# Second feed-forward product as seven block products per unit, and a token-major output projection

## The chip, the cores and the metric

One core of one Trainium2 chip runs the whole layer as one program. The metric is the device time in microseconds (us) of that program; lower is better. The engines are TensorE (PE in the profile; PEld its weight loads), VectorE (DVE), ScalarE (ACT), GpSimd (POOL) and SyncE (SP), which issues most of the DMAs.

## The reference

The layer takes x (512 tokens by 1024 features, float32) and 25 weight tensors. Cut to what matters here:

```python
h = x * (1 + sc1) + sh1                      # modulation from c, w_ada
p = h @ w_in                                 # pool, RWKV and gate columns
y_pool = pool_branch(p_pool, ...); y_rwkv = rwkv7_branch(p_rwkv, ...)
g_pool, g_rwkv = split(sigmoid(p_gate))
mixed = (g_pool * y_pool + g_rwkv * y_rwkv) @ w_out
x = layer_norm(ALPHA * x + (1 + gt1) * mixed, ln1_g, ln1_b)
h = x * (1 + sc2) + sh2
f = square(relu(h @ w_ff1)) @ w_ff2          # 1024 -> 4096 -> 1024
x = layer_norm(ALPHA * x + (1 + gt2) * f, ln2_g, ln2_b)
```

## The kernel before, in words

Activations lie feature-major in SBUF: 128 features on the partitions, 512 tokens (S) along the free axis, KT = 8 such tiles for 1024 features. Float32 precision is made from three products of a reduced format: each operand is split into a high part (ScalarE copies it to the format) and a low part (value minus high part), and hi x hi, hi x lo and lo x hi are added in one PSUM bank. So one column block of 128 outputs over 1024 inputs is 8 x 3 = 24 matmuls of 128 x 512.

The weights come in chunks k = 0, 1, ... of 128 x (8 x 128), 512 KB each, listed in `srcs`. For each chunk SyncE issues the load into `w_raw` (`load_chunk`, L401), ScalarE writes `w_hi` (`split_hi`, L641, and `split_again`, L942), GpSimd writes `w_lo` (`split_lo`, L560, L616), TensorE multiplies (`product`, L1773), and the semaphores `w_in*`, `hi_ready`, `lo_ready`, `w_used` carry it along; three or four slots are used in turn. K_UP is the first chunk behind the scan, K_OUT the first of w_out, K_FF the first of the feed-forward part.

Every engine works through its own instructions in the order written; each instruction also raises a semaphore that its own engine then waits for (`link`). The stages, one after the other:

- The input projection and the chunked RWKV scan, QUADS rounds of 27 slots (to about 520 us). At its end VectorE makes y.
- Mixing: for each of 8 column blocks the gate columns, the RWKV up product and the pool up product; VectorE combines them in four operations and splits off `mix_lo`. Before the first block come four small `mix_pool` matmuls, which wait for ScalarE's `pool_scaled`.
- The output projection, feature-major: 8 blocks of 24 matmuls (w_out is the stationary operand). x is loaded again (`x_again`) and turned to feature-major by 32 transposes between the blocks; `take_product` adds gate times product to `res`, and VectorE and ScalarE sum values and squares as they come.
- First layer norm over features, thus over partitions: matmuls with a matrix of ones give the sums (`token_sums`, L1837), `spread` (L1854) brings mean and deviation back to all partitions, VectorE subtracts and multiplies (L1356, L1357), ScalarE makes h and its high part (L932, L933), GpSimd the low part (L611). `first_products` (L1875) starts on it.
- Feed-forward, four quarters q of 1024 hidden features: 8 chunks of w_ff1 give 8 hidden tiles (ScalarE: relu L951, high part of the square L952; VectorE: square L1371 and low part L1373), then 8 chunks of w_ff2 multiply them, and VectorE adds gate times product to `res` (L1378). The middle quarters are a loop.
- In the last quarter each finished tile of `res` is turned back to token-major (`turn_back`, L1761), ScalarE copies it out (L959), VectorE takes statistics, and the second layer norm is applied in token-major (L1404, L1406; one of the four token blocks by ScalarE and GpSimd). Four stores of 512 KB end the program.

## Time and profile before

| | us |
|---|---|
| median of 3 runs | 1096.57 |
| lowest, highest | 1090.94, 1103.49 |
| profiled execution: its own time | 1097.87 |
| profiled execution: span of the instructions | 1096.1 |
| TensorE busy in the span | 995.9 |
| VectorE, ScalarE, GpSimd busy | 520.8, 413.7, 402.4 |

The span runs from the first to the last instruction of the profiled execution; the time also holds what lies around it. Busy times of matmuls overlap, since each one is pipelined behind the other, so the spacing of their starts tells the rate. DVE, ACT and POOL rows name the instruction's line, the tile written and the tiles read; "set" and "bank" are PSUM.

### The profile page before, as it was taken

The numbers are of one execution on the slowest core, as the hardware profiler recorded it, in microseconds if no ns is written. First come the engines' busy times: TensorE is split into PE (matmuls) and PEld (weight loads), VectorE is DVE, ScalarE is ACT, GpSimd is POOL, SyncE is SP. The second block draws the span as 40 slices with busy tenths as digits, with TensorE's granted clock in tenths as the row PEclk, the third lists the DMA queues.
The fourth block names the chain that finished last, engine by engine and source line by source line (L and its number), as shares of the span: only waits on it lengthen the run. The fifth ranks groups of instructions, "written<-read, shape, count | busy, mean of one in ns | idle before, by whom it ended". The sixth has DMA issues, their size and how long they took to land.

```text
span 1096.1 us, 25425 instructions
## 1 busy us (share of the span) xinstructions
PE 995.9 (91%) x10997; PEld 798.7 (73%) x10997; DVE 520.8 (48%) x620; ACT 413.7 (38%) x500; POOL 402.4 (37%) x236
## 2 busy tenths in 40 slices
PE   1798999798989899899899999899999999999992
PEld 1676777685768578766688888678888888888881
DVE  5735688466837867853431246745112112112217
ACT  0336355345435623335432224384124224214311
POOL 6332512310231131125454444355444444443422
PEclk9698999998999999999999999889999999999996
DMA  9332333233222423422443543304333333333201
GB/s 363 103 90 62 97 102 100 61 83 119 86 79 80 119 65 99 116 86 59 135 115 87 165 123 96 96 5 130 97 96 97 96 96 96 96 96 96 77 1 77
DMA packets 153641, 108.08 MB, mean 99 GB/s; under 512 B 5395, under 2 KB 145601, under 8 KB 153537
## 3 DMA queue, kind: packets, MB, share of 16 engines
q1 hardware_dynamic: 143729, 83.46, 26.0%
q10 hardware_dynamic: 9808, 23.08, 6.9%
q8 instruction: 84, 1.38, 0.5%
q14 instruction: 20, 0.16, 0.0%
HBM read 100.23 MB, written 2.10 MB: 93 GB/s over the span
## 4 chain that ended last, share of the span: by engine, by line
PE 75%; DVE 14%; ACT 3%; DMA 2%; issue 2%; POOL 1%; ACTq 1%; SPq 1%; DVEq 0%; POOLq 0%
PE set L1773 23%; PE bank L1773 20%; PE bank L1476 12%; PE set L1518 3%; PE set L1530 2%; PE set L1542 2%; PE bank L1457 2%; PE set L1554 1%; PE bank L1875 1%; DMA ptab<-in_mu_shift_dram 1%; DVE y L1280 1%; DVE Q L1038 1%; PE set L1565 1%; DVE Q L1057 1%; PE set L1875 1%
## 5 line engine op out<-in xcount | busy, mean ns | idle before, releaser
L560 POOL TENSOR_TENSOR w_lo<-w_raw,w_hi 128x1024 fp32r<-128x1024 f32 (+2 forms) x87 | 201.7, 2318 | 441.2 <-ACT w_hi L641 401.1
L616 POOL TENSOR_TENSOR w_lo<-w_raw,w_hi 128x1024 fp32r<-128x1024 f32 x48 | 115.8, 2412 | 145.6 <-ACT w_hi L942 145.4
L1476 PE MATMUL bank<-h_hi,w_hi 128*128 128x512 f32 x256 | 109.3, 427 | 2.2 <-POOL w_lo L560 2.0
L669 ACT ACTIVATE Q<-set 128x1024 f32<-128x1024 f32 x56 | 57.4, 1025 | 135.1 <-PE set L1530 75.6
L641 ACT ACTIVATE w_hi<-w_raw 128x1024 fp32r<-128x1024 f32 (+2 forms) x75 | 75.5, 1006 | 83.0 <-PE set L1773 43.5
L942 ACT ACTIVATE w_hi<-w_raw 128x1024 fp32r<-128x1024 f32 x60 | 63.7, 1061 | 110.7 <-PE bank L1773 53.9
L1476 PE MATMUL bank<-h_lo,w_hi 128*128 128x512 f32 x256 | 104.1, 407 | 0.0
L1476 PE MATMUL bank<-h_hi,w_lo 128*128 128x512 f32 x256 | 103.5, 404 | 0.6 <-issue 0.6
L1371 DVE TENSOR_TENSOR f<-t 128x512 f32<-128x512 f32 x32 | 26.3, 823 | 125.6 <-ACT t L951 125.2
L1773 PE MATMUL set<-y_hi,w_hi 128*128 128x512 f32 x192 | 76.2, 397 | 0.0
L1773 PE MATMUL bank<-h_hi,w_hi 128*128 128x512 f32 x192 | 75.9, 395 | 0.0
L1773 PE MATMUL bank<-h_hi,w_lo 128*128 128x512 f32 x192 | 75.3, 392 | 0.0
L1773 PE MATMUL bank<-h_lo,w_hi 128*128 128x512 f32 x192 | 75.3, 392 | 0.0
L1773 PE MATMUL set<-y_lo,w_hi 128*128 128x512 f32 x192 | 75.3, 392 | 0.0
L1773 PE MATMUL set<-y_hi,w_lo 128*128 128x512 f32 x192 | 75.1, 391 | 0.0
L1476 PEld LDWEIGHTS bank<-h_hi,w_hi 128*128 128x128 f32 x256 | 49.9, 195 | 19.2 <-issue 6.0
L1530 PE MATMUL set<-Q 64*64 64x64 f32 x2560 | 45.7, 224 | 14.8 <-issue 7.0
L1476 PEld LDWEIGHTS bank<-h_hi,w_lo 128*128 128x128 f32 x256 | 49.6, 194 | 11.1
L1530 PEld LDWEIGHTS set<-Q 64*64 64x64 f32 x2560 | 42.6, 138 | 20.5 <-issue 13.0
L1476 PEld LDWEIGHTS bank<-h_lo,w_hi 128*128 128x128 f32 x256 | 49.8, 194 | 9.0
L1773 PE MATMUL bank<-y_hi,w_hi 128*128 128x512 f32 x128 | 50.9, 398 | 0.0
L1773 PE MATMUL bank<-y_hi,w_lo 128*128 128x512 f32 x128 | 50.2, 393 | 0.0
(338 smaller groups left out, 2028.7 us busy)
## 6 DMA issues: line engine op xcount, KB each, us to landing
w_raw<-in_w_ff_dram SPq DMA_DIRECT2D x64, 512.0 KB, 3.9
w_raw<-in_w_in_dram SPq DMA_DIRECT2D x46, 512.0 KB, 3.8
y<-in_w_ada_dram ACTq DMA_DIRECT2D x20, 512.0 KB, 4.2
ada<-in_w_ada_dram SPq DMA_DIRECT2D x16, 512.0 KB, 10.0
Q<-in_w_ada_dram ACTq DMA_DIRECT2D x12, 512.0 KB, 4.3
w_raw<-in_w_rwkv_up_dram SPq DMA_DIRECT2D x8, 512.0 KB, 4.1
w_raw<-in_w_out_dram SPq DMA_DIRECT2D x8, 512.0 KB, 4.0
xtok<-in_x_dram SPq DMA_DIRECT2D x4, 512.0 KB, 10.0
```

The costliest lines, as they stand in the source:

```text
L560: link(pool.tensor_tensor(part_of(k, w_lo), part_of(k, w_raw), part_of(k, w_hi).bitcast(F32), ALU.subtract), "lo_ready")
L616: again(pool.tensor_tensor(part_of(k, w_lo), part_of(k, w_raw), part_of(k, w_hi).bitcast(F32), ALU.subtract), "lo_ready")
L641: link(act.activation(part_of(k, w_hi), part_of(k, w_raw), ACT.Copy), "hi_ready")
L669: link(act.activation(by_half(tile), psum_flat(set_of(name)), ACT.Copy), "act_kept")
L942: link(act.activation(part_of(k, w_hi), part_of(k, w_raw), ACT.Copy), "hi_ready")
L1371: link(dve.tensor_tensor(f3[:, :], r[:, :], r[:, :], ALU.mult))
L1457: mm = pe.matmul(o, w, hx, start=(m == 0), stop=(m == 3 * KT - 1))
L1476: mm = pe.matmul(o, w, hx, start=(m == 0), stop=(m == 3 * KT - 1))
L1518: mm = pe.matmul(ps[C * q:C * q + C, p, c * C:(c + 1) * C], by_head(left, p, q, c), by_head(right, p, q, c - back), start=(m == 0), stop=( ...
L1530: mm = pe.matmul(ps[N * p:N * p + N, q, c * C:(c + 1) * C], by_pair(left, p, q, c), by_pair(right, p, q, c), start=(m == 0), stop=(m == le ...
L1542: mm = pe.matmul(ps[C * q:C * q + C, p, 2 * c * C:2 * (c + 1) * C], by_head(left, p, q, HC * h + c), two_blocks(x, z, rows, q, HC * h + c) ...
L1773: mm = pe.matmul(o, w[chunks[k][1]][:, kt, :], hx[:, kt, :], start=(kt == 0 and m == 0), stop=(kt == kts - 1 and m == 2))
```

## The change

The hidden features come in 8 units u of 512 (NU) in place of 4 quarters of 1024. A unit multiplies A (512 tokens by 512 hidden) by B (512 hidden by 1024 outputs), each cut into 2 x 2 blocks: A into blocks of 256 x 256, B into B11, B12, B21, B22 of 256 x 512. In place of eight block products it makes seven, by the scheme of Strassen and Winograd: with T1 = B12 - B11, T3 = B22 - B12, T2 = B22 - T1, T4 = B21 - T2 on the weight side (VectorE, `summed`) and four sums of activation blocks (`a_sums`). Each block product is 2 rows of 128 tokens x 2 blocks of 128 hidden features x 3 terms = 12 matmuls, with the activations stationary and 512 columns of weights moving, so the result is token-major. Some products open a PSUM bank, others add onto it (`OPENS`), and VectorE adds the bank into `acc_out` at up to two points (`take`, 14 per unit).

The splitting is shared differently. Per unit ScalarE makes 11 high parts; the low parts of chunks 0, 1 and of the last four products (m = 7 to 10) are GpSimd's, those of chunks 2, 3 and products 0 to 2 (`low_tile`) VectorE's, which also makes the low parts of the activation blocks (`lows`).

The output projection becomes token-major too: `mix_hi` and `mix_lo` are stationary and w_out moves, in two halves z of 512 columns with four chunks each. Its weights are first multiplied by the first gate (`scaled_out`), which `spread_gate` brought onto all partitions as a row at the end of the scan. x is added without turning; the first layer norm is taken with bn_stats along the free axis, and the normalised x is turned to feature-major for h. The norm's gain and bias for the residual are applied block by block in units 0 to 2 (`residual`), the second gate and the final addition in unit 6 (`merged`), and in the last unit the weights carry the gate, so that the products are added straight to `res`. The result needs no turning back. More raw weight buffers exist, and the first chunks behind the scan are loaded before y is ready.

The core of the diff; the mirror definitions of buffers, the loops' counting and the removed functions are left out:

```diff
+        FORMS = ("B11", "B21", "T2", "T1", "T3", "B22", "T4")
+        NFORM = len(FORMS)
+        QUARTERS = dict(B11=(3, 0, 0), B12=(4, 0, 1), B21=(5, 1, 0), B22=(6, 1, 1))
+        FORM_RAW = dict(B11=3, B21=5, T2=3, T1=8, T3=4, B22=6, T4=5)
...
+        NU = DFF // (4 * P)
+        PER = 4 + NFORM
+        K_FORM = K_FF + 4
+        srcs += [w_cols(w_ff1, m * P) for m in range(4)] + [None] * NFORM
...
+        SLOT = (2, 0, 1, 3, 2, 0, 1, 3, 2, 0, 1)
...
+
+            raw, i, z = QUARTERS[name]
+            if u:
+                wait_low(sp, 4 + FORMS.index(LAST_FORM[name]), u - 1)
+                if name == "B11":
+                    sp.wait_ge(sem("summed"), NSUM * u)
+            elif name == "B22":
+                sp.wait_ge(sem("w_used"), K_PU[KT - 1] + 1)
+            else:
+                sp.wait_ge(sem("lo_ready"), K_OUT + {"B11": 6, "B12": 7, "B21": 5}[name] + 1)
+            src = w_ff2[0, (4 * u + 2 * i) * P:(4 * u + 2 * i + 2) * P, z * S:(z + 1) * S].rearrange("(i p) f -> p i f", p=P)
+            sp.dma_start(two_by(w_raw[raw]), src).then_inc(sem(f"w_in{raw}"), 16)
...
+        PRODUCTS = ((0, 4), (2, 0), (5, 4), (4, 6), (1, 4), (6, 6), (3, 4))
+        OPENS = (True, True, False, True, False, False, False)
+        FREED_BY = (6, None, 0, 5, 2, 3, 4)
+        READ_INTO = ((0, 0), (0, 0), (0, 1), (2, 1), (2, 1), (0, 1), (2, 0))
+        FIRST_READ = (0, 2, 3, 6)
+        OUT_BANKS = ((4, 5, 0, 1), (2, 3, 6, 7))
+        SUMS = ("T1", "T3", "T2", "T4")
+        NSUM = len(SUMS)
+        A_READY = ((1, 3), (2, 4), (5, 7), (5, 7), (6, 8), (6, 8), (6, 8))
...
+        LO_BY_DVE = (2, 3, 4, 5, 6)
+        QUARTER_ORDER = ("B11", "B12", "B22", "B21")
...
+            for k in (K_UP, K_UP + 1):
+                load_chunk(sp, k)
             sp.wait_ge(sem("y_ready"), QUADS)
...
+            load_chunk(sp, K_UP + 2)
+            for o in range(2):
+                load_out(sp, o)
...
+            for o in range(3, 6):
+                load_out(sp, o)
+            for m in (2, 0):
+                load_chunk(sp, K_FF + m)
+            load_out(sp, 6)
+            load_chunk(sp, K_FF + 1)
+            load_out(sp, 7)
+            load_chunk(sp, K_FF + 3)
+            load_quarter(sp, 0, "B22")
+            sp.wait_ge(sem("pu_taken"), KT)
+            for at, src in enumerate((ln1_g, ln1_b, ln2_g, ln2_b)):
+                sp.dma_start(ln_rows[:, at, :], src.to_broadcast([P, D])).then_inc(sem("rows_in"), 16)
+            for name in ("B21", "B11", "B12"):
+                load_quarter(sp, 0, name)
...
+            with pool.Fori(0, NU - 1) as q:
+                again = loop_link(pool, counts, q, {"lo_ready": 6}, "pool_step")
+                for m in (0, 1, 7, 8, 9, 10):
+                    pool.wait_ge(sem("hi_ready"), q * PER + (K_FF + PER + m + 1))
+                    raw = w_raw[CHUNK_RAW[m] if m < 4 else FORM_RAW[FORMS[m - 4]]]
+                    again(pool.tensor_tensor(w_lo[SLOT[m]][:, :, :], raw[:, :, :], w_hi[SLOT[m]][:, :, :].bitcast(F32), ALU.subtract), "lo_ready")
...
+                        for z, one in enumerate((gate1, gate2)):
+                            act.wait_ge(sem("gate_spread"), z + 1)
+                            link(act.activation(one[:, :], pset[(1, 0)[z]][:, :, :].rearrange("p g t -> p (g t)"), ACT.Copy, scale=(0.5, 1.0)[z]),
+                                 "gate_rows")
...
+
+            def normalise(j, stage):
+
+                act.wait_ge(sem("ln_cols"), 2 * stage + j // 2 + 1)
+                link(act.activation(res[:, j, :], res[:, j, :], ACT.Identity, scale=small[:, 36 + j:37 + j], bias=small[:, 40 + j:41 + j]), "x_hat")
+
+            root(0, 0)
+            normalise(0, 0)
+            normalise(1, 0)
+            root(1, 0)
...
+            for m in range(4):
+                relu_of(link, m, 0, 0)
+                high_raw(link, m)
+                high_sums(link, m)
+                split_hi(K_FORM + m)
...
+                x0, x1 = left[:, i, 0:S // 2], left[:, i, S // 2:S]
+                if n % 4 < 2:
+                    link(dve.tensor_tensor(a_sum[:, 0, :], x0, x1, ALU.subtract), "a_summed")
+                else:
+                    link(dve.tensor_tensor(a_sum[:, 1, :], x1, right(n)[:, S // 2:S], ALU.add))
+                    link(dve.tensor_tensor(a_sum[:, 2, :], a_sum[:, 1, :], x0, ALU.subtract))
+                    link(dve.tensor_tensor(a_sum[:, 3, :], right(n)[:, 0:S // 2], a_sum[:, 2, :], ALU.subtract), "a_summed")
...
+                raw, slot = w_raw[CHUNK_RAW[m] if m < 4 else FORM_RAW[FORMS[m - 4]]], SLOT[m]
+                link(dve.tensor_tensor(w_lo[slot][:, :, :], raw[:, :, :], w_hi[slot][:, :, :].bitcast(F32), ALU.subtract), "lo_by_dve")
...
+            def take(link, unit, at, row, units=0, into=None):
+
+                into = into or acc_out
+                wait_half(unit, at, row, units)
+                j, z = READ_INTO[at][0] + row, READ_INTO[at][1]
+                product = bank[PRODUCTS[at][1] + row]
+                if unit == 0 and at in FIRST_READ:
+                    link(dve.tensor_copy(part(into, j, z), product), "taken")
+                else:
+                    link(dve.tensor_tensor(part(into, j, z), product, part(into, j, z), ALU.add), "taken")
...
+            def merged(j, z):
+
+                link(dve.tensor_tensor(part(acc_out, j, z), part(acc_out, j, z), gate2[:, z * S:(z + 1) * S], ALU.mult))
+                link(dve.tensor_tensor(part(res, j, z), part(res, j, z), part(acc_out, j, z), ALU.add))
...
+            def residual(j, z):
+
+                link(dve.tensor_tensor(part(res, j, z), part(res, j, z), part(ln_rows, 0, z), ALU.mult))
+                link(dve.tensor_tensor(part(res, j, z), part(res, j, z), part(ln_rows, 1, z), ALU.add))
...
+                link(dve.tensor_tensor(part(res, j, z), bank[OUT_BANKS[z][j]], part(res, j, z), ALU.add), "out_taken")
+                statistics(j, z)
...
+                for at in range(NFORM):
+                    for row in range(2):
+                        take(link, unit, at, row, units)
+                    if between:
+                        between(at)
...
+            def residuals(of):
+
+                def between(at):
+                    if at in (0, 2, 4) and 3 * of + at // 2 < len(parts):
+                        residual(*parts[3 * of + at // 2])
+
+                return between
...
+            def unit_sums(link, units, last=False):
+
+                low_tile(link, 2, 1, units)
+                low_tile(link, 3, 1, units)
+                if last:
+                    for name in QUARTER_ORDER:
+                        loaded(name, 1, units)
+                        scaled_tile(QUARTERS[name][0], QUARTERS[name][2], gate2)
+                summed(link, "T1", 1, units)
+                summed(link, "T3", 1, units)
+                for m in range(4):
+                    dve.wait_ge(sem("hidden_raw"), units * 4 + (4 + m + 1))
+                    lows(link, 4 + m, units)
+                    if m == 0:
+                        low_tile(link, 4, 1, units)
+                    if m == 1:
+                        summed(link, "T2", 1, units)
+                        low_tile(link, 5, 1, units)
+                    if m == 2:
+                        low_tile(link, 6, 1, units)
+                        summed(link, "T4", 1, units)
+
+            for u in (1, 2):
+                unit_sums(link, u - 1)
+                takes(link, 1, u - 1, residuals(u))
...
+            def merges_before(at):
+                if at in (1, 4):
+                    for row in range(2):
+                        merged(READ_INTO[at][0] + row, READ_INTO[at][1])
+
+            takes(link, 1, NU - 3, merges_before)
+            unit_sums(link, NU - 2, True)
+            for at in range(NFORM - 1):
+                for row in range(2):
+                    take(link, 1, at, row, NU - 2, res)
+                if at < 4:
+                    merged(*((0, 1), (1, 1), (2, 0), (3, 0))[at])
+                if at in (1, 4, 5):
+                    for row in range(2):
+                        statistics(READ_INTO[at][0] + row, READ_INTO[at][1])
+            spreads(0)
+            for row in range(2):
+                take(link, 1, NFORM - 1, row, NU - 2, res)
+                statistics(2 + row, 0)
+                if row == 0:
+                    columns(0, 1)
...
+            def spread_gate(z, first):
+
+                for f in range(KT):
+                    mm = pe.matmul(pset[z][:, f // 4, f % 4 * P:(f % 4 + 1) * P], mod[:, first + f:first + f + 1].to_broadcast([P, P]), ident[:, :],
...
+            def quarters(unit, free, units=0):
+
+                for at, (form, first) in enumerate(PRODUCTS):
+                    wait_low(pe, 4 + at, unit, units)
+                    w = [two_by(half[SLOT[4 + at]]) for half in (w_hi, w_lo)]
+                    for row in range(2):
+                        free(at, row)
+                        if at and FREED_BY[at] is not None and FREED_BY[at] < at:
+                            pe.wait_ge(sem("taken"), units * (2 * NFORM) + (2 * NFORM * unit + 2 * FREED_BY[at] + row + 1))
+                        for i in range(2):
+                            if row == 0:
+                                pe.wait_ge(sem("a_low"), units * 8 + (8 * unit + A_READY[form][i]))
+                            for m, (a, wx) in enumerate(((a_hi, w[0]), (a_lo, w[0]), (a_hi, w[1]))):
+                                mm = pe.matmul(bank[first + row], a[:, form, i, row * P:(row + 1) * P], wx[:, i, :],
+                                               start=OPENS[at] and i == 0 and m == 0, stop=i == 1 and m == 2, skip_group_check=True)
+                        if row == 0:
+                            mm.then_inc(sem("half_made"), 1)
+                    mm.then_inc(sem("w_used"), 1)
...
+            for kt in range(KT):
+                pe.wait_ge(sem(("h2_lo_by_dve", "h2_lo_by_pool")[kt % 2]), kt // 2 + 1)
+                if kt < 4:
                     for j in range(TB):
-                        mm = pe.transpose(bank[6 + f % 2][:, j * P:(j + 1) * P], x_again[:, j, f * P:(f + 1) * P], ident[:, :])
+                        mm = turn(kt + 4, j)
...
+                slot = SLOT[m]
+                wait_low(pe, m, base, units)
+                for kt in range(KT):
+                    for at, (w, hx) in enumerate(((w_hi, h2_hi), (w_hi, h2_lo), (w_lo, h2_hi))):
+                        mm = pe.matmul(bank[m][:, :], w[slot][:, kt, :], hx[:, kt, :], start=(kt == 0 and at == 0),
+                                       stop=(kt == KT - 1 and at == 2))
+                mm.then_inc(sem("w_used"), 1)
```

## Rows read from the trace of the kernel before

**Rows 1.** the page: busy time, the chain by engine, a feed-forward weight load
```profile
PE 995.9 (91%) x10997; PEld 798.7 (73%) x10997; DVE 520.8 (48%) x620; ACT 413.7 (38%) x500; POOL 402.4 (37%) x236
...
PE 75%; DVE 14%; ACT 3%; DMA 2%; issue 2%; POOL 1%; ACTq 1%; SPq 1%; DVEq 0%; POOLq 0%
...
w_raw<-in_w_ff_dram SPq DMA_DIRECT2D x64, 512.0 KB, 3.9
```

**Rows 2.** busy time by stretch: us; busy (instructions) per engine; granted clock; DMA share, GB/s
```profile
735.00:1032.00 297.00, 297.00 (x1291) 242.66 (x1290) 69.44 (x87) 97.12 (x118) 134.63 (x56) 1.00 0.34 98
```

**Rows 3.** the chain that ended last: start us, us, what; feed-forward part
```profile
734.44 11.05 PE set L1773 x48
...
900.32 11.04 PE bank L1773 x48
```

**Rows 4.** the timeline of VectorE (DVE) and GpSimd (POOL): start us, us, instruction [idle before]
```profile
714.05 0.69 DVE L1356 TENSOR_TENSOR G<-G,set 128x512 f32<-128x512 f32 x1
...
713.56 1.27 POOL L611 TENSOR_TENSOR h_lo<-t,h_hi 128x512 fp32r<-128x512 f32 x1 [6.01 <-ACT h_hi L933]
...
738.26 2.61 POOL L616 TENSOR_TENSOR w_lo<-w_raw,w_hi 128x1024 fp32r<-128x1024 f32 x1 [0.21 <-ACT w_hi L942]
...
738.63 2.78 DVE L1373 TENSOR_TENSOR y_lo<-f,y_hi 128x512 fp32r<-128x512 f32 x1
```

**Rows 5.** the timeline of TensorE from the output projection to the first chunks
```profile
649.85 0.39 PE L1773 MATMUL set<-mix_hi,w_hi 128*128 128x512 f32 x1
...
698.29 0.39 PE L1773 MATMUL bank<-mix_hi,w_lo 128*128 128x512 f32 x1
...
705.51 2.06 PE L1854 MATMUL set<-ident,small 128*128 128x128 f32 x8
...
714.98 0.77 PE L1875 MATMUL set<-h_hi,w_hi 128*128 128x512 f32 x1 [3.92 <-POOL h_lo L611]
715.54 0.63 PE L1875 MATMUL set<-h_lo,w_hi 128*128 128x512 f32 x1
715.97 0.63 PE L1875 MATMUL set<-h_hi,w_lo 128*128 128x512 f32 x1
```

**Rows 6.** busy time and granted clock (PEclk) by slices, columns as in rows 2
```profile
704.00:706.00 2.00, 2.00 (x10) 2.00 (x11) 0.20 (x2) 1.06 (x1) 0.79 (x1) 0.50 0.00 0
...
720.00:722.00 2.00, 2.00 (x10) 1.60 (x9) 1.20 (x2) 1.90 (x4) 1.78 (x2) 0.88 0.00 0
```

**Rows 7.** the timeline of ScalarE (ACT) and TensorE at the pool mixing
```profile
533.57 1.06 ACT L641 ACTIVATE w_hi<-w_raw 128x1024 fp32r<-128x1024 f32 x1 [8.11 <-DMA w_raw<-in_w_rwkv_up_dram]
...
536.12 1.10 PE L1796 MATMUL set<-sg,wmix 128*128 128x512 f32 x2 [1.28 <-ACT lnv L882]
538.61 1.10 PE L1796 MATMUL set<-t,wmix 128*128 128x512 f32 x2 [1.40 <-ACT lnv L882]
```

**Rows 8.** groups by line and shape: count, busy us, mean ns, idle before
```profile
L616 POOL TENSOR_TENSOR w_lo<-w_raw,w_hi 128x1024 fp32r<-128x1024 f32 x48 | 115.8, 2412 | 145.6 <-ACT w_hi L942 145.4 <-POOL w_lo L616 0.2
...
L942 ACT ACTIVATE w_hi<-w_raw 128x1024 fp32r<-128x1024 f32 x60 | 63.7, 1061 | 110.7 <-PE bank L1773 53.9 <-PE set L1773 52.5 <-ACT y_hi L952 3.8
...
L951 ACT ACTIVATE t<-set 128x512 f32<-128x512 f32 x16 | 9.6, 598 | 50.0 <-PE set L1773 43.9 <-DVE y_lo L1373 3.8 <-PE set L1875 2.3
...
L1192 DVE TENSOR_TENSOR O<-O,gn 128x1024 f32<-128x1024 f32 x3 | 3.7, 1224 | 0.1
```

**Rows 9.** the timeline of TensorE at a group that turns back, last quarter
```profile
1038.21 0.60 PE L1761 MATMUL set<-ident,G 128*128 128x128 f32 x4
1038.56 0.48 PE L1773 MATMUL bank<-y_hi,w_hi 128*128 128x512 f32 x1
```

**Rows 10.** the timeline of TensorE and VectorE at the end
```profile
1073.91 0.40 PE L1773 MATMUL set<-y_hi,w_lo 128*128 128x512 f32 x1
...
1083.93 3.24 DVE L1404 SCALAR_TENSOR_TENSOR xt<-xt,small,acc 128x1024 f32<-128x1024 f32 x1
...
1091.81 1.28 DVE L1406 SCALAR_TENSOR_TENSOR xt<-xt,small,ada_late 128x1024 f32<-128x1024 f32 x1
```

727 lines of the change are left out of this document (415 added, 312 removed).

## Prediction

> **What bounds the kernel now.** I read the page first: TensorE is busy 91% of the span, and the chain that ended last lies on it for 75% [rows 1]. Then the stretches: in the 297 us from 735 it never rests [rows 2]; the timeline shows it without products only from 698.5 to 715 us (the first layer norm) and after 1074 us (the second). In the feed-forward part one piece of the chain follows another, 48 matmuls in 11.05 us, 0.2302 us each [rows 3]. So a matmul saved there is worth its whole 0.23 us, as long as the other engines feed TensorE as evenly as now. VectorE and GpSimd have room (69 and 135 us busy in those 297) [rows 2], but not independent room. A VectorE instruction of 128x512 takes 0.69 us with one operand in PSUM, and keeps that beside a running GpSimd instruction (714.05). With both operands in SBUF it took 2.78 us when it began while GpSimd ran a w_lo subtraction (738.63): it ended 0.54 us after GpSimd's. They take turns, one instruction each [rows 4]. That pair of rows decides the forecast.
>
> **The change, part by part** (base: the profiled run, 1097.87 us, span 1096.1; the median of the three runs is 1.3 below it).
>
> Scan's end: +1.0. TensorE gets 16 matmuls of 128 columns that spread two gates over the partitions. Eight such take 2.06 us at half clock [rows 5, 6], so 16 cost 2.1 (full clock) to 4.2. ScalarE's two copies of 128x1024 (1.06 each) delay y by up to as much, under the gate product. Against it, loading K_UP's weights before the wait for y takes away the DMA that ends ScalarE's wait of 8.1 us, behind which the pool mixing was late and TensorE idle 1.28 + 1.40 = 2.7 us [rows 7]. Net -0.6 to +1.5; I take +1.0, since the gate product now also waits for the first copy. Weights scaled by the first gate (8 VectorE products of 1.2 us, [rows 8] for the size) fit beside mixing, whose four VectorE operations need 2.8 of 8.3 us per column block.
>
> Output projection: -4.5. 192 matmuls stay; the 32 transposes of x and the mean's matmul leave it. It took 649.85 to 698.52, 48.7 us [rows 5]; 192 x 0.2302 = 44.2.
>
> First norm: -6.3. Now 698.52 to 714.98, 16.5 us without a product [rows 5]. After: last take 0.7 and its statistics 0.7, but ScalarE reaches the first root only after the high part of K_FF+1, which waits for the last projection matmul, so VectorE stands behind that root before the last take (+1.3); two aggregations, root, columns 1.3; the last block's normalisation 0.8; transposes 0.5, two scalings out of PSUM 1.5, high part 0.6, low part 0.7; ten hand-overs of about 0.1; ScalarE's three normalisations (1.1 to 1.3 each by the row of 128x1024 [rows 8]) lie beside it. 10.2 us.
>
> Second product: -22.1. Per unit of 512 hidden features 7 block products x 12 matmuls = 84 in place of 96; 8 units save 96 matmuls x 0.2302. The moving operand stays 512 columns wide. The page "TensorE: Matmul & The Clock Gate" of the Trainium skill, section "Wait — 56ns, not 53.3ns?", gives 215.7 ns between such matmuls at full clock; by that the saving would be 20.7 us and the sum 1.4 higher. The trace's own spacing is used.
>
> Transposes: -1.3. Each group of four costs 0.35 us, and 0.09 at the next matmul, which shows 0.48 in place of 0.39 [rows 9]; seven leave the last quarter, four come into the first chunks.
>
> Stalls in the units: +33.2. These come from laying the units' instructions out engine by engine, in the order of the code, with the durations of [rows 4, 8]. TensorE needs 22.1 us for four hidden chunks and 19.3 for seven products. Let E be the end of chunk 3. ScalarE's work per unit is 11 x 1.06 + 8 x 0.6 + 4.2 = 21 us, and fits. VectorE: 5 low tiles and 4 weight sums at 1.25, 8 differences of 128x256 at 0.45 (0.69 for 512 columns and 1.22 for 1024 leave 0.42 for 256), the low parts 5.2, 14 takes from PSUM at 0.72: 30 us of 41.4, of which 20 need SBUF twice, and GpSimd's six w_lo need 14.4 more of the same turn-taking. Four places come out late:
> (1) product 1 needs the low part of chunk 3: relu and square 0.6 each, three differences 1.35, low part 0.69 and hand-overs and the next matmul's start make about 4.1 us after E; TensorE has 15 matmuls to do until then, 3.45. Late by 0.7, in each of seven units, 2.2 in the first, where two chunks end together: 6.3.
> (2) units 0 to 2 carry two residual operations behind products 0, 2 and 4. GpSimd starts its four w_lo at E+5.4. VectorE ends the takes of product 0 at E+6.8; its first residual operation waits until E+7.9, the second until E+10.6; so the take of product 2, for which product 4 waits (same banks), is done at E+13.4, and product 4 was due at E+11.7. Late 1.7, and the same again at product 5, 1.8: 10.4 in three units.
> (3) unit 6 has four operations (gate and residual) between the takes of products 1 and 2, each behind one of GpSimd's: the take of product 2 ends at E+18, 6.3 late.
> (4) unit 7: scaling four weight quarters by the gate adds 4 x 1.25 us before T1. Behind unit 6's late takes VectorE begins 2.4 us after chunk 0 does, has 22.2 us of work before the differences of chunk 3 and waits 4 for ScalarE's high parts, so product 1 is 5.3 late; product 4 then waits 4.9 for takes behind merging: 10.2.
> Both ends: if nothing of this reached TensorE, 0; if GpSimd's turns fell as in (2) in all units, 5 x 3.5 more.
>
> Clock: +4.8. Granted clock is 1.00 until 702 us and 0.50 from 704, after the projection's matmuls had ended at 698.5, and 0.88 again in the slice from 720, dense matmuls having begun at 715 [rows 5, 6]. Those are the levels 2.4 and 1.2 GHz. At the low one matmuls start 0.43 us apart in place of 0.23 (715.54, 715.97) [rows 5]; 12 of them cost 2.4 us. The first chunks pay this now and after. The waits of 6.3 in unit 6 and 5.3 in unit 7 leave TensorE with nothing at all; I count one such fall behind each, 4.8; if the clock holds, 0.
>
> Tail: -1.3. Now the last matmul starts at 1073.91 and VectorE's last operation ends at 1093.1, with 3 us of storing behind it; the final scaling is six VectorE operations, two of them 3.24 us beside GpSimd's two [rows 10]. After, only a take, statistics of one block and the root stand before the same scaling, but takes arrive two products late: 20.4 against 21.7 us.
>
> DMA: the same 64 loads of 512 KB. Three w_ff2 quarters and four broadcast rows (2 MB) fall into the projection; a load takes 3.9 us [rows 1], so they land before T1. Its bound: if B12 were late by a load, +3.9.
> Waits: a block row of 6 matmuls has up to four semaphore waits at its head where the present loop has two per 24 matmuls, at no cost (48 matmuls in 11.05 in the loops too [rows 3]); nearest row for a price is the 0.09 us after a transpose group [rows 9]: 0 to 112 block rows x 0.09 = 10 us. I take 0.
>
> Sum: 1.0 - 4.5 - 6.3 - 22.1 - 1.3 + 33.2 + 4.8 - 1.3 = +3.5: 1101.4 on the profiled run's scale, 1100 on the median's.
>
> **Rivals.**
> *The turns cost nothing* (0.27). VectorE works 30 of 41 us, and if the residual and merging operations fall between GpSimd's, only (1), 6.3, and perhaps 4 in the last unit stay: 33.2 + 4.8 becomes about 10, time 1072. For it: takes come first in VectorE's order, and GpSimd is free half the time. Against: GpSimd's four w_lo stand back to back exactly in the products' phase, and [rows 4] show what an SBUF operation does then.
> *VectorE becomes the bound in all units* (0.26), slower. If VectorE's low tiles and sums at the head of a unit also meet GpSimd's two w_lo of chunks 0 and 1, each meeting adds up to 2.1 us to a phase with 19.7 us of VectorE work in 22.1. It decides from the point where the low part of chunk 3 is more than 3.45 us behind the matmul. 3.5 us in the five plain units: +17, time 1117. For it: the sum 19.7 + 4.8 is over 22.1. Against: GpSimd's pair is mostly done while takes run.
> The page "SBUF — State Buffer" of the Trainium skill, section "Who interferes with whom", speaks against the change here: a VectorE instruction with two SBUF inputs and a GpSimd one that reads SBUF lock each other out for a whole instruction. By it the first of these rivals would need luck in the order and the second only density. The trace agrees (2.78 against 0.69 us).
> *The saving isn't had* (0.05): the waits at each block row cost their 10 us: 1110.
>
> **How the numbers follow.** Forecast case 0.42, its own range 1088 to 1111 (stalls 33 within a third). A change within 1% of 1097, 11 us, can hardly be told from none. Faster by over 1% (below 1085.6) is the first rival and a little of the forecast: 0.30. Slower by over 1% (above 1107.5): the second, half the third, and the upper end of the forecast: 0.29. Same: 0.41. The range 1071 to 1116 leaves out the ends of both rivals.
>
> **What would show it.** Right: TensorE's matmuls in the feed-forward part fewer by 96 at 0.23 us spacing; idle before products 1, 4 and 5 with VectorE as releaser; GpSimd's and VectorE's 128x512 SBUF operations at 2.5 to 2.8 us in products' phases; unit times near 46 us for units 0 to 2, 42 for 3 to 5, about 50 for 6 and 7; about 10 us between projection and first chunk. Wrong: units of 41.5 us throughout (first rival), idle before products 1 in units 3 to 5 over 3 us (second), or spacing above 0.24 at the heads of block rows (third). A late T1, seen as VectorE waiting for DMA before it takes the projection's second half, would add to the first norm.

## The result and the profile after

The changed kernel takes 1109.72 us (median of 4; 1107.87 to 1111.28) beside 1096.05 for the kernel before on the same chip: ratio 1.0112, interval 1.0079 to 1.0146. By the ratio it is 12 us slower (9 to 16), where the forecast had 3.5. Its profiled run took 1108.20 us, with a span of 1106.3. First the page: busy time by engine, then the chain that ended last by engine.

```profile
PE 976.2 (88%) x10851; PEld 776.2 (70%) x10851; DVE 717.3 (65%) x862; ACT 462.1 (42%) x561; POOL 362.8 (33%) x218
...
PE 61%; DVE 26%; ACT 6%; issue 3%; DMA 2%; POOL 1%; ACTq 1%; SPq 0%; DVEq 0%; POOLq 0%
```

Beside [rows 1] TensorE has 20 us less to do, as intended, and VectorE 197 us more. VectorE's part of the chain went from 14% to 26%: the kernel now waits for it at places. The windows of single units show where (stretch, its length, busy time and instructions of PE, PEld, DVE, ACT, POOL, then granted clock, DMA share, GB/s).

```profile
757.00:803.00 46.00, 42.36 (x181) 33.48 (x181) 37.86 (x46) 21.13 (x28) 14.81 (x7) 1.00 0.30 92
849.00:891.50 42.50, 41.82 (x181) 33.73 (x180) 29.12 (x39) 21.22 (x27) 14.38 (x7) 1.00 0.30 89
976.60:1026.00 49.40, 42.35 (x174) 33.71 (x173) 39.01 (x42) 21.24 (x27) 13.33 (x6) 0.93 0.27 83
1026.00:1085.00 59.00, 48.14 (x187) 37.72 (x185) 55.00 (x65) 19.10 (x25) 12.86 (x5) 0.88 0.00 0
```

Unit 1, with six residual instructions, needs 46.0 us; unit 3, without, 42.5; nearly all of the difference is idle time of TensorE (3.6 against 0.7 us), which does the same matmuls. In the last window VectorE is busy 55 of 59 us. The timeline of TensorE names each wait, in brackets, with what ended it.

```profile
736.95 0.50 PE L2142 MATMUL bank<-w_hi,a_hi 128*128 128x512 f32 x1 [1.97 <-DVE a_lo L1481]
...
792.47 0.49 PE L2142 MATMUL set<-w_hi,a_hi 128*128 128x512 f32 x1 [1.49 <-DVE acc_out L1550]
...
797.01 0.51 PE L2142 MATMUL set<-w_hi,a_hi 128*128 128x512 f32 x1 [1.51 <-DVE acc_out L1550]
...
916.76 0.40 PE L2142 MATMUL bank<-w_lo,a_hi 128*128 128x512 f32 x1
917.83 0.50 PE L2142 MATMUL bank<-w_hi,a_hi 128*128 128x512 f32 x1 [0.68 <-DVE a_lo L1481]
...
1017.19 0.79 PE L2142 MATMUL set<-w_hi,a_hi 128*128 128x512 f32 x1 [6.04 <-DVE acc_out L1550]
1017.77 0.63 PE L2142 MATMUL set<-w_hi,a_lo 128*128 128x512 f32 x1
1018.20 0.63 PE L2142 MATMUL set<-w_lo,a_hi 128*128 128x512 f32 x1
...
1058.46 0.79 PE L2142 MATMUL bank<-w_hi,a_hi 128*128 128x512 f32 x1 [5.04 <-DVE a_lo L1481]
...
1073.42 0.79 PE L2142 MATMUL set<-w_hi,a_hi 128*128 128x512 f32 x1 [5.48 <-DVE res L1550]
```

These are the four places of the forecast: product 1 behind the low part of hidden chunk 3 (a_lo), products 4 and 5 behind takes, product 4 of unit 6, and products 1 and 4 of unit 7. Behind the two waits at product 4 the granted clock is at its lower level:

```profile
1018.00:1021.00 3.00, 3.00 (x8) 2.35 (x8) 1.90 (x3) 0.00 (x0) 0.00 (x0) 0.50 0.02 8
1074.00:1078.00 4.00, 4.00 (x11) 3.16 (x10) 3.79 (x7) 0.00 (x0) 0.00 (x0) 0.50 0.00 0
```

What holds VectorE is seen in its timeline beside GpSimd's.

```profile
787.39 2.78 DVE L1560 TENSOR_TENSOR res<-res,ln_rows 128x512 f32<-128x512 f32 x1
790.20 1.42 DVE L1550 TENSOR_TENSOR acc_out<-bank,acc_out 128x512 f32<-128x512 f32 x2
...
786.96 2.65 POOL L731 TENSOR_TENSOR w_lo<-w_raw,w_hi 128x1024 fp32r<-128x1024 f32 x1 [0.16 <-POOL w_lo L731]
```

The residual's addition began at 787.39 during GpSimd's subtraction, which ended at 789.61, and lasted 2.78 us; the two takes behind it, with an operand in PSUM, take 0.71 each. It is the pattern of [rows 4]. In unit 6 three of the first four merging instructions last 2.70 to 2.74 us.

**By stretches.** Marks are starts of the same matmuls in the two profiles [rows 5, 10], so each line is a difference of rows:

| stretch | before | after | change | forecast |
|---|---|---|---|---|
| until the scan's last input product ends | 516.16 | 514.49 | -1.7 | - |
| from there to the output projection | 133.69 | 133.82 | +0.1 | +1.0 |
| output projection | 48.67 | 44.33 | -4.3 | -4.5 |
| first norm, to the first chunk's first matmul | 16.46 | 12.75 | -3.7 | -6.3 |
| feed-forward, to the last matmul's end | 359.16 | 379.10 | +19.9 | +14.6 |
| from there to the span's end | 21.96 | 21.81 | -0.1 | -1.3 |

The first line is no more than scatter: in the changed kernel and its ten experiments the instructions up to the output projection are the same, and it began anywhere from 646.0 to 653.2 us in their profiles. So a single profile is read from a mark: below, "from the mark" counts from the first matmul of the output projection to VectorE's last operation, 443.2 us before (649.85 to 1093.09) and 453.7 after (648.31 to 1101.97). One part scatters behind the mark too: the first chunk starts 57.1 us behind it in every run whose first norm is unchanged, but unit 0 then takes 51.2, 51.0, 50.7 or 50.2 us in runs that do the same there (changed kernel; 3 and 4; 7; 8), as the granted clock rises and falls at different times. So a difference of 1 us can't be read from this number alone.

### The profile page after: what moved, and what is told of

It reads as the page before. It is cut to its first block, busy times and chain, and to the rows that moved or that the text cites. A ratio compares the mean times of both kernels' runs of the same rounds, so it can differ in the third digit from the quotient of the medians.

```text
span 1106.3 us, 25836 instructions
## 1 busy us (share of the span) xinstructions
PE 976.2 (88%) x10851; PEld 776.2 (70%) x10851; DVE 717.3 (65%) x862; ACT 462.1 (42%) x561; POOL 362.8 (33%) x218
## 4 chain that ended last, share of the span: by engine, by line
PE 61%; DVE 26%; ACT 6%; issue 3%; DMA 2%; POOL 1%; ACTq 1%; SPq 0%; DVEq 0%; POOLq 0%
PE bank L1797 12%; PE set L2142 7%; PE bank L2214 6%; PE set L2099 6%; PE bank L2099 5%; PE set L2214 3%; PE set L2167 3%; PE set L1839 2%; PE set L1851 2%; PE set L1863 2%; DVE w_lo L1501 2%; DVE acc_out L1550 2%; PE bank L1778 1%; DVE y L1448 1%; PE set L1875 1%
## 5 line engine op out<-in xcount | busy, mean ns | idle before, releaser
L1797 PE MATMUL bank<-h_hi,w_hi 128*128 128x512 f32 x256 | 109.7, 429 | 2.1 <-POOL w_lo L668 2.0
L1797 PE MATMUL bank<-h_lo,w_hi 128*128 128x512 f32 x256 | 104.3, 407 | 0.0
L1797 PE MATMUL bank<-h_hi,w_lo 128*128 128x512 f32 x256 | 103.6, 405 | 0.4 <-issue 0.4
L2142 PE MATMUL set<-w_hi,a_hi 128*128 128x512 f32 x192 | 78.6, 409 | 19.1 <-DVE acc_out L1550 12.1
L2142 PE MATMUL set<-w_hi,a_lo 128*128 128x512 f32 x192 | 77.4, 403 | 0.0
L2142 PE MATMUL set<-w_lo,a_hi 128*128 128x512 f32 x192 | 77.1, 402 | 0.0
L1550 DVE TENSOR_TENSOR acc_out<-set,acc_out 128x512 f32<-128x512 f32 x76 | 52.6, 692 | 23.4 <-PE set L2142 21.4
L1501 DVE TENSOR_TENSOR w_lo<-w_raw,w_hi 128x1024 fp32r<-128x1024 f32 x38 | 46.6, 1226 | 10.3 <-ACT w_hi L1113 7.6
L2214 PE MATMUL set<-h_hi,w_hi 128*128 128x512 f32 x128 | 50.6, 396 | 0.0
L2214 PE MATMUL set<-h_lo,w_hi 128*128 128x512 f32 x128 | 50.2, 392 | 0.0
```

Source lines behind the costliest of these rows:

```text
L1501: link(dve.tensor_tensor(w_lo[slot][:, :, :], raw[:, :, :], w_hi[slot][:, :, :].bitcast(F32), ALU.subtract), "lo_by_dve")
L1550: link(dve.tensor_tensor(part(into, j, z), product, part(into, j, z), ALU.add), "taken")
L1797: mm = pe.matmul(o, w, hx, start=(m == 0), stop=(m == 3 * KT - 1))
L2142: mm = pe.matmul(bank[first + row], a[:, form, i, row * P:(row + 1) * P], wx[:, i, :], start=OPENS[at] and i == 0 and m == 0, stop=i == 1 ...
L2214: mm = pe.matmul(bank[m][:, :], w[slot][:, kt, :], hx[:, kt, :], start=(kt == 0 and at == 0), stop=(kt == KT - 1 and at == 2))
```

## Experiments

Each is the changed kernel with one edit, unless said otherwise. Ratios are to the kernel before, run on the same chip; the changed kernel's is 1.0112 (1.0079 to 1.0146).

**1. Same instructions' time, one operand.**

```diff
             def residual(j, z):
-                link(dve.tensor_tensor(part(res, j, z), ..., part(ln_rows, 0, z), ALU.mult))
-                link(dve.tensor_tensor(part(res, j, z), ..., part(ln_rows, 1, z), ALU.add))
+                for _ in range(2):
+                    link(dve.bn_stats(stat[:, 2 * j + z, :], res[:, j, z * S:(z + 1) * S]))
```

> The sixteen residual instructions of units 0 to 2 (two SBUF operands, 0.69 us alone) are replaced in their places by sixteen bn_stats of the same 128x512 block, which also last 0.69 us and read one operand; the scale and the row of the first norm are so left out of the residual. Theory (turn-taking: a VectorE instruction with two SBUF operands alternates with GpSimd's 2.4 us ones): the two waits of 1.5 us at products 4 and 5 of units 0 to 2 go, these units come every 42.6 us like 3 to 5, and the time falls by 10 to 10.5 us, to about 1099. Rival (VectorE simply has 1.4 us more to do behind three products, whatever the operands): unit spacing stays near 46 us and the time at 1110.

Measured: 1098.54 us, ratio 1.0012 (0.9997 to 1.0028); from the mark 444.6, 9.1 less. Unit spacings are 42.50, 42.53, 42.53 where they were 46.1 in units 1 and 2. VectorE's timeline at the place of the residual:

```profile
787.14 1.42 DVE L1560 BATCH_NORM_STATS2 stat<-res 128x6 f32<-128x512 f32 x2
...
786.56 2.41 POOL L731 TENSOR_TENSOR w_lo<-w_raw,w_hi 128x1024 fp32r<-128x1024 f32 x1 [0.16 <-ACT w_hi L1113]
```

Two instructions in 1.42 us beside GpSimd, against 2.78 us for one. VectorE is given the same time of work; the form of the operands decides. The rival is out. (bn_stats also writes only six values a row; that this isn't the reason is seen at the takes, which write all 512, read one operand from PSUM and one from SBUF, and keep 0.71 us beside GpSimd.) The page "SBUF — State Buffer" of the Trainium skill, section "Who interferes with whom", says that a VectorE instruction with at most one SBUF input doesn't contend with GpSimd outside its two-port modes; the trace agrees.

**2. Same instructions, another place.** `takes` of units 0 to 2 lose `residuals(...)`; units 1 to 4 are written out and get two pairs each:

```diff
                     if m == 2:
                         low_tile(link, 6, 1, units)
                         summed(link, "T4", 1, units)
+                    if m < len(rest):        # rest: two (j, z) parts in units 1 to 4
+                        residual(*rest[m])
```

> All sixteen residual instructions are kept but stand behind VectorE's low parts of block forms 0 and 1 in the hidden phases of units 1 to 4, two pairs a unit, where GpSimd has nothing for 26 us and VectorE idles 2.1 and 1.5 us. Theory (place beside GpSimd, not the amount of work): as without them, units 0 to 2 every 42.6 us, total about 1099. Rival (VectorE is short of time in the whole unit): the 1.4 us each return as a longer wait at product 1 of units 1 to 4, 2 to 3 us instead of 0.65, and the time stays at 1106 to 1110.

Measured: 1098.29 us, ratio 0.9998 (0.9974 to 1.0023); from the mark 443.9, 9.8 less. Units 1 to 5 come every 42.5 us, and product 1 waits 0.64, as in units 1 and 2 before. In unit 1:

```profile
768.39 0.69 DVE L1559 TENSOR_TENSOR res<-res,ln_rows 128x512 f32<-128x512 f32 x1
769.12 0.69 DVE L1560 TENSOR_TENSOR res<-res,ln_rows 128x512 f32<-128x512 f32 x1
770.38 0.42 DVE L1468 TENSOR_TENSOR a_sum<-left 128x256 f32<-128x256 f32 x1 [0.57 <-ACT left L1089]
```

The whole residual costs nothing where GpSimd rests: VectorE still waits 0.57 us for ScalarE behind it.

**3. Unit 7 without scaling.** ScalarE's wait for the scaled quarters leaves too; the gate is missing on unit 7's share.

```diff
-                if last:
-                    for name in QUARTER_ORDER:
-                        loaded(name, 1, units)
-                        scaled_tile(QUARTERS[name][0], QUARTERS[name][2], gate2)
```

> VectorE's four multiplications of the last unit's weight quarters by the gate row (5.0 us together) are left out, and with them the gate on that unit's part of the output. Theory: the wait of 5.0 us at product 1 of unit 7 falls to 0.7, its clock fall goes too; but the merges then meet more of GpSimd's low parts, so that the wait at product 4 grows from 5.5 to 7 or 8; the time falls by 4 to 5 us to 1105. Rival (the two waits are independent, as the sum of the prediction had them): product 4 keeps 5.5 and the time falls by 7 us to 1103.

Measured: 1106.55 us, ratio 1.0059 (1.0024 to 1.0093); from the mark 448.5, 5.2 less. TensorE in unit 7, then VectorE's first long merging addition and GpSimd's subtraction beside it:

```profile
1057.30 0.50 PE L2136 MATMUL bank<-w_hi,a_hi 128*128 128x512 f32 x1 [0.66 <-DVE a_lo L1479]
...
1072.24 0.79 PE L2136 MATMUL set<-w_hi,a_hi 128*128 128x512 f32 x1 [7.07 <-DVE res L1548]
...
1061.62 2.79 DVE L1553 TENSOR_TENSOR res<-res,acc_out 128x512 f32<-128x512 f32 x1
...
1061.19 2.66 POOL L731 TENSOR_TENSOR w_lo<-w_raw,w_hi 128x1024 fp32r<-128x1024 f32 x1 [0.16 <-POOL w_lo L731]
```

The same two in the changed kernel, where product 1 starts at 1058.46 and product 4 at 1073.42:

```profile
1062.76 2.78 DVE L1555 TENSOR_TENSOR res<-res,acc_out 128x512 f32<-128x512 f32 x1
...
1062.33 2.66 POOL L731 TENSOR_TENSOR w_lo<-w_raw,w_hi 128x1024 fp32r<-128x1024 f32 x1 [0.16 <-POOL w_lo L731]
```

The first wait gives 4.4 us, the second takes 1.6 back. The two are not independent, and the rival, which took them so, is out by the 7.07 us (the time alone would not tell: the ratio's interval holds both forecasts). But the reason given before the run is not what the rows show: the merges meet GpSimd exactly as before. The long addition begins 4.32 us behind product 1 here and 4.30 in the changed kernel, and product 4 starts 14.94 us behind product 1 here and 14.96 there. VectorE sets this distance. TensorE, at full clock behind the short wait, is only 1.6 us sooner at product 4 and waits that much longer. It is 14.95 or 14.96 us in runs 1, 2, 5, 7 and 8 too, though the slow matmuls behind product 1 cost between 1.7 and 2.7 us in them: in this kernel the clock's fall behind product 1 costs nothing by itself.

**4. All merging late in unit 7.**

```diff
-            takes(link, 1, NU - 3, merges_before)
+            takes(link, 1, NU - 3)
...
-                if at < 4:
-                    merged(*((0, 1), (1, 1), (2, 0), (3, 0))[at])
+                for j, z in {3: ((0,0),), 4: ((1,0),(2,1),(3,1)), 5: ((0,1),(1,1),(2,0),(3,0))}.get(at, ()):
+                    merged(j, z)
...                                                  # the statistics of these parts move behind them
```

> The eight merging instructions of unit 6 are taken out of it; all sixteen stand in unit 7, two behind product 3, six behind product 4, eight behind product 5, where GpSimd has nearly finished. Theory: the waits of 6.0 us (unit 6, product 4) and 5.5 us (unit 7, product 4) go with their clock falls, and since unit 6 hands over on time the wait at product 1 of unit 7 falls from 5.0 to 1.5; the last matmul comes 14 to 15 us earlier, VectorE's tail grows by 3 to 5; the time falls by 10 us to 1099.5. Rival (the work is only pushed into the end, where nothing hides it): the sixteen at 0.69 lengthen the end by as much as the waits give, and the time stays at 1108 to 1112.

Measured: 1102.24 us, ratio 1.0032 (1.0006 to 1.0059). TensorE ends 22.2 us sooner from the mark (414.1 against 436.3), VectorE only 8.6 (445.1). The 22.2 are the waits (6.04 + 5.48, and 5.04 down to 1.27: 15.3) and the slow matmuls behind three of them (2.1 + 1.9 + 2.9). Both theories had a part. The waits go, and TensorE gains 22.2 us where 14 to 15 were expected; but from TensorE's end to VectorE's it is now 31.0 us instead of 17.3, 13.7 more where 3 to 5 were expected. Fifteen of the sixteen merging instructions take 0.69 us there.

**5 and 6. The sum T4 earlier, or later.** In both places where it is made (here for experiment 5; in 6 it moves to `m == 3`):

```diff
                     if m == 1:
                         summed(link, "T2", 1, units)
                         low_tile(link, 5, 1, units)
+                        summed(link, "T4", 1, units)
                     if m == 2:
                         low_tile(link, 6, 1, units)
-                        summed(link, "T4", 1, units)
```

> VectorE forms the weight sum T4 one chunk earlier (after the low part of form 1 instead of form 2), where it idles 1.5 us, so that it is free 0.5 us sooner for the low parts of hidden chunk 3. Theory (the 0.65 us wait at product 1 is VectorE's queue, ending in T4): the wait falls to about 0.2 in units 1 to 6; unit 7, where VectorE is full, keeps its 5 and 5.5 us or more; the time falls by 0 to 3 us to 1107 to 1109.5. Rival (the wait is the chain from TensorE over ScalarE to VectorE, whatever stands before): 0.65 stays, and so does 1109.7.

> The same sum T4 is put behind the low parts of hidden chunk 3. One would expect the wait at product 1 to go and 4 to 5 us with it (rival: 1105). Theory: product 1's wait does fall to 0.2, but VectorE takes product 0 out 1.25 us later, and product 2 needs that bank: a new wait of about 1.2 us in front of product 2 in every unit, 0.7 us more a unit than before, in all 3 to 4 us slower than the changed kernel, 1113.

Measured: earlier 1103.18 us, ratio 1.0040 (1.0012 to 1.0068), from the mark 449.6, 4.0 less; later 1107.73, ratio 1.0095 (1.0057 to 1.0134), from the mark 456.3, 2.7 more. The ratio of the second can't be told from the changed kernel's; its timeline can. TensorE in unit 3, first with T4 earlier, then later:

```profile
873.36 0.50 PE L2142 MATMUL bank<-w_hi,a_hi 128*128 128x512 f32 x1 [0.15 <-DVE a_lo L1481]
```

```profile
879.76 0.50 PE L2144 MATMUL bank<-w_hi,a_hi 128*128 128x512 f32 x1 [0.15 <-DVE a_lo L1481]
...
883.03 0.49 PE L2144 MATMUL set<-w_hi,a_hi 128*128 128x512 f32 x1 [0.92 <-DVE acc_out L1550]
```

Both take the wait at product 1 from 0.68 to 0.15. Later, a wait of 0.92 stands before product 2, whose bank waits for a take: spacing 43.2 instead of 42.55. Earlier, nothing takes its place until unit 7: spacing 42.0. The wait was VectorE's queue; its rival is out. Of the 4.0 us less, 1.0 lies in unit 0, which takes 50.2 us for 51.2, as it also does in run 8, where it isn't changed: 3.0 are left, the upper end of the 0 to 3 expected. In run 6 the naive gain is out, and the loss is under the 3 to 4 us expected: the new wait is 0.92 for 1.2.

**7. GpSimd after the first norm.**

```diff
-            for k in range(K_UP, K_FF + 2):
+            for k in range(K_UP, K_FF + 1):
                 split_lo(k)
+            pool.wait_ge(sem("last_x_hat"), 1)
+            split_lo(K_FF + 1)
```

> GpSimd's low part of the second weight chunk of the first product waits until VectorE has normalised the last rows of the first norm. Theory (a VectorE instruction of 128x2 elements with SBUF operands waited 1.8 us for GpSimd's 2.34 us one): it lasts 0.17 us instead of 1.96, everything behind it in the first norm comes 1.5 to 1.8 us earlier, TensorE's pause between the output projection and the first turn falls from 6.4 to 6.4 with the last rows' turn 1.8 earlier, the time falls by 1.5 to 1.8 to 1108. Rival (the rows' way over ScalarE is as long, or the chunk's low part now comes late): the first chunk starts when it did, or later by up to 2 us: 1109.7 to 1112.

The changed kernel first (VectorE, GpSimd, then TensorE), then this one:

```profile
694.51 1.96 DVE L1577 SCALAR_TENSOR_TENSOR small<-small 128x2 f32<-128x2 f32 x1
...
694.12 2.34 POOL L668 TENSOR_TENSOR w_lo<-w_raw,w_hi 128x1024 fp32r<-128x1024 f32 x1 [3.18 <-ACT w_hi L760]
...
699.23 1.09 PE L2174 MATMUL set<-ident,res 128*128 128x128 f32 x4 [6.42 <-ACT res L1068]
```

```profile
697.03 0.16 DVE L1579 SCALAR_TENSOR_TENSOR small<-small 128x2 f32<-128x2 f32 x1
...
701.48 2.35 POOL L668 TENSOR_TENSOR w_lo<-w_raw,w_hi 128x1024 fp32r<-128x1024 f32 x1 [8.03 <-DVE res L1625]
...
699.94 1.08 PE L2176 MATMUL set<-ident,res 128*128 128x128 f32 x4 [4.62 <-ACT res L1070]
```

Measured: 1107.54 us, ratio 1.0087 (1.0057 to 1.0117), which alone can't be told from the changed kernel's; from the mark 451.1, 2.6 less. The first chunk starts 55.28 us after the mark instead of 57.08: exactly the 1.8 us that the instruction of two columns lost, and TensorE's pause falls by as much, from 6.42 to 4.62. The other 0.8 lie in units 0 and 6, which the edit doesn't touch.

**8. The end without GpSimd.** GpSimd's two lines for block 0 leave; the stores go in the order 2, 1, 0, 3.

```diff
-                    link(dve.tensor_tensor(res[:, 1, :], res[:, 1, :], ln_rows[:, 2, :], ALU.mult))
-                    link(dve.tensor_tensor(res[:, 1, :], res[:, 1, :], ln_rows[:, 3, :], ALU.add), "out_ready1")
+                    for i in (1, 0):
+                        link(dve.tensor_tensor(res[:, i, :], res[:, i, :], ln_rows[:, 2, :], ALU.mult))
+                        link(dve.tensor_tensor(res[:, i, :], res[:, i, :], ln_rows[:, 3, :], ALU.add), f"out_ready{i}")
```

> At the end of the kernel VectorE does the row multiplication and addition of row block 0 too (2.5 us), GpSimd nothing, and the stores go out in the order of the blocks' completion. Theory (GpSimd's two instructions of 2.34 us lengthen two of VectorE's by 1.7 and 2.2 us): VectorE ends 1.4 to 1.9 us earlier in spite of its two added instructions, the stores start earlier; the time falls by 1.5 to 2.5 us to 1107.5. Rival (two engines share the work): one engine alone needs 2.5 us more: 1112.

Measured: 1104.22 us, ratio 1.0063 (1.0038 to 1.0087); from the mark 451.7, 2.0 less. Of the 2.0, 0.3 lie before product 4 of unit 7, where nothing is changed, and 1.6 behind it. The span ends 3.0 us behind VectorE instead of 4.3; the stores no longer leave together. The changed kernel's two lines, and this one's:

```profile
1090.12 1.90 DVE L1577 SCALAR_TENSOR_TENSOR small<-small 128x2 f32<-128x2 f32 x1
1092.05 3.44 DVE L1721 SCALAR_TENSOR_TENSOR res<-res,small,ln_rows 128x1024 f32<-128x1024 f32 x1
```

```profile
1087.24 0.16 DVE L1574 SCALAR_TENSOR_TENSOR small<-small 128x2 f32<-128x2 f32 x1
1087.44 1.28 DVE L1718 SCALAR_TENSOR_TENSOR res<-res,small,ln_rows 128x1024 f32<-128x1024 f32 x1
```

One engine doing all of it is faster than two in turns: GpSimd's 4.7 us held VectorE for 3.9, and VectorE needs 2.5 for the same: 1.4 us, and 1.3 at the stores.

**9 and 10. All moves together**: 2, 5, 7, 8, and the merges either spread (9: behind products 2 and 6 of unit 6, in unit 7's hidden phase, behind its product 4) or late as in 4 (10). The spread ones:

```diff
-                if at in (1, 4):                       # unit 6
-                    for row in range(2):
-                        merged(READ_INTO[at][0] + row, READ_INTO[at][1])
+                if at in (2, 6):
+                    merged(at // 6, 0)
...
+                    if last and m < 2:                 # unit 7, hidden phase
+                        for j, z in (((2, 1),), ((3, 1), (0, 1)))[m]:
+                            merged(j, z)
...
-                if at < 4:                             # unit 7, products
-                    merged(*((0, 1), (1, 1), (2, 0), (3, 0))[at])
+                if at == 4:
+                    for j, z in ((1, 1), (2, 0), (3, 0)):
+                        merged(j, z)
```

> All moves that keep the computation, together: residual in the hidden phases of units 1 to 4, T4 one chunk earlier, GpSimd after the first norm, the end without GpSimd; the eight merges spread over both units (two behind products 2 and 6 of unit 6, three in the hidden phase of unit 7, three behind its product 4). From the single runs, counted from the start of the output projection to VectorE's last operation (453.7 us in the changed kernel): -9.8 residual, -4.0 T4, -2.0 first norm, -2.0 end, and -8.6 or a little more for the merges, less 1 to 2 that some of them share: 428 to 430 us, the time near 1084, 1.1 to 1.5% under the kernel before. Rival (VectorE, now full from unit 7 on, is the same bound for several of the moves, so they don't add): 436 to 440 us, 1093.

> The same, with all merges late in unit 7 as in the run of that name. By the laying-out of the units VectorE ends 1 to 3 us later than with the spread merges though TensorE ends earlier; rival: TensorE's end decides, and this one is 3 to 5 us faster.

Measured: spread 1081.81 us, ratio 0.9856 (0.9827 to 0.9884), from the mark 429.0; late 1082.58 us, ratio 0.9883 (0.9852 to 0.9914), from the mark 428.6. Both are within the 428 to 430 expected. Late, TensorE ends 9.9 us sooner than spread (399.0 against 408.9), and from the mark VectorE seems to end at the same time. But the two are the same program up to unit 6, and their unit 0 took 49.2 us (spread) and 46.6 (late): in the spread one the slow matmuls lasted longer at its start and came again behind its wait of 2.02 us, which they did not in the other, behind 2.01. Counted from the start of unit 7, VectorE ends after 70.7 us (spread) and 73.0 (late), 2.3 later though TensorE is earlier, as the theory had it; its rival is out. The two times don't differ beyond their intervals. With the spread ones TensorE still waits in unit 7:

```profile
1033.23 0.50 PE L2147 MATMUL bank<-w_hi,a_hi 128*128 128x512 f32 x1 [2.60 <-DVE a_lo L1480]
...
1037.99 0.79 PE L2147 MATMUL bank<-w_hi,a_hi 128*128 128x512 f32 x1 [3.80 <-DVE a_lo L1480]
```

So the changed kernel's plan is worth having once VectorE's work stands away from GpSimd's: 1.4% faster than the kernel before (1.2 to 1.7%). The greater part of it comes from the token-major output projection and the first norm behind it: from the mark to the first chunk it takes 55.3 us for 65.1, 9.9 less. From the first chunk to the end of the span, where the seven block products stand, it is 376.7 us spread and 376.4 late for 381.1, 4.4 and 4.7 less, of 22.1 us of matmuls saved. In the changed kernel itself these two stretches were 8.0 us less and 19.8 more. No run has one of the two changes without the other. Part of the gain, the end without GpSimd, isn't owed to the plan at all: the kernel before has a slow instruction, of 3.24 us, at that place too [rows 10].

## Why the forecast was right, and where its sum was short

**Right: the likeliest case.** The saving in matmuls is lost to VectorE in turns with GpSimd. Runs 1 and 2 show the mechanism (form and place, not amount). Units 1 and 2 took 46.1 us, 3 to 5 42.5 and 6 51.0, where 46, 42 and about 50 stood. Units 0 and 7 took 51.2 and 57.1, where 46 and about 50 stood; but the prediction's own terms add up to about 51 and 54 for them, so it was the list of signs that was wrong there more than the sum. TensorE's idle time in front of products adds up to 30.5 us (3.6, 3.6, 3.7, three times 0.7, 7.1, 10.5) against 33.2; only in unit 0 is a wait missing, its product 4, as slow matmuls before it had used that time (in runs 5 and 8, without slow matmuls there, it stands: 1.56 us). The first rival (1072) and the second (five plain units 3.5 us longer) don't occur: the plain units wait 0.68, once. The third, waits at heads of block rows: unit 4 runs 180 matmuls in 42.5 us, of which the one late place takes 0.9, so the other heads cost under 0.2 us together.

**Right: output projection** (-4.3 for -4.5) and the scan's end (+0.1 for +1.0, within its range): the spreading matmuls took 3.73 us, and TensorE's 2.7 us idle at the pool mixing [rows 7] are gone.

**Short by 8.4 us** (11.9 by the stretches behind the first line, for 3.5):
- *Clock, +4.8*: the step "I count one such fall behind each" of two waits failed. The clock fell four times, behind waits of 1.97 us (unit 0), 6.04, 5.04 and 5.48; the windows 1018 to 1021 and 1074 to 1078 show 0.50 granted. The slow matmuls behind them (0.43 apart) cost 1.9, 2.1, 1.9 and 2.9: 8.7, of which 1.0 is the restart counted next. +2.9. Nor do falls and waits simply add up: the one behind product 1 of unit 7 only used time that TensorE would have waited at product 4 (run 3).
- *Stalls, +33.2*: the waits were sized by TensorE's idle time. A wait costs more: at 917.83 0.68 idle is 0.84 us late (916.76 to 917.83 in place of 0.23), and the matmul after it is late 0.1 more. 15 waits x 0.26 = 3.9, less the 2.7 by which the idle time was overestimated: +1.2. That leaves about 1.2 of the feed-forward part's 5.3 unexplained; a plain unit takes 0.13 to 0.18 us more than its matmuls, its wait and the 0.26, and there are eight.
- *First norm, -6.3*: the step left GpSimd out, though the forecast's own rule covers it. A VectorE instruction on two columns waited behind GpSimd's low part: 1.8 of the 2.6 missing (run 7). The sum was also wrong in itself: the durations that it lists add up to 9.1 us, and 10.2 stood; so 3.7 us were missing from its terms, and the slip hid 1.1 of them. ScalarE's last normalisation, which it had "beside" VectorE's, ended 0.5 us behind it (701.12), and the transposes waited for it; from there to the first scaling out of PSUM (702.19) it was 1.0 us where the transposes were put at 0.5; and four more transposes keep the first product back by 0.8:

```profile
701.17 2.82 PE L2174 MATMUL set<-ident,res 128*128 128x128 f32 x12 [0.86 <-ACT res L1068]
...
704.63 1.11 PE L2174 MATMUL set<-ident,res 128*128 128x128 f32 x4 [0.63 <-DVE h_lo L1631]
705.39 0.78 PE L2203 MATMUL bank<-h_hi,w_hi 128*128 128x512 f32 x1
```

- *Tail, -1.3*: VectorE ends 17.5 us behind the last matmul's end (its start and 0.23) for 18.95 before, but the stores start within 3 us of each other and end 4.3 us behind it for 3.0: +1.2 (run 8 takes that back).

**The chances.** The measured time lies at the edge between "same" and "slower by over 1%", which had 0.29. But take the second rival's 0.26 and half the third's 0.05 from that, and 0.005 is left for the forecast case itself to end above 1107.5, where its own range went to 1111. The likeliest case came true in the corner to which the chances gave next to nothing.

In short: where the forecast laid the instructions out in order, with the turns, it was right to 3 us in 33; where it only added durations, in the first norm, it missed a turn and mis-added its terms.

## What to carry to other kernels

Work "spread over the idle time" of VectorE must be placed by GpSimd's timetable, not by VectorE's share of busy time: sixteen instructions cost 10 us in one phase and none some 20 us earlier in a unit. Look even at two-column instructions on a chain, and at the end of a kernel, where splitting the last work over the two engines made it longer. In this kernel a wait of TensorE costs its idle time plus 0.26 us, plus 1.5 to 2.9 us where the granted clock falls behind it, unless another wait for the same VectorE follows and takes that up. A single profile is to be compared from a mark behind the common part, and stretch by stretch: of a difference "from the mark", a part can lie where the edit changes nothing. And two changes made together want a line each: here the stretch of one gave 8 us and that of the other took 20, and the sum showed neither.

## What the runs showed of the hardware that wasn't expected

The exclusion doesn't depend on size: 128x2 elements waited 1.96 us instead of 0.16. It does depend on the form: bn_stats of an SBUF block kept 0.71 us beside GpSimd's subtraction. And the clock fell behind a wait of only 1.97 us in unit 0, while no wait of 1.5 us was followed by slow matmuls. A wait of about 2 us doesn't always bring it down: of the ten profiles with one of 1.97 to 2.02 there, seven show slow matmuls behind it (the changed kernel, runs 1 to 4, 7 and 9) and three show none (5, 8 and 10); nor did any follow the 2.60 us in unit 7 of run 9. What decides it was not tried.
